# Sixteen small SBUF to SBUF copies on two queues in place of a trip through DRAM, in a hybrid attention step

## The reference, cut to what matters

```
z = h @ w_in                                   # split into q, k, v, gate of both mixers
s = einsum('bqhcd,bshcd->bhcqs', q, k) / sqrt(64)
p = softmax(s)
p = p[:, :, 0] - lam * p[:, :, 1]              # one block of probabilities for a head
o = einsum('bhqs,bshe->bqhe', p, v)            # then RMS norm, gate, and o @ w_out
```

## Time and profile before

| | |
|---|---|
| median of 3 runs | 1240.4 us (1240.19 to 1240.67) |
| the profiled execution: its time, its span | 1241.58 us, 1239.8 us |
| granted TensorE clock, mean | 0.995 |
| TensorE busy | 1205.5 us, 97% of the span |
| VectorE, ScalarE, GpSimd busy | 824.4, 595.7, 259.4 us (66%, 48%, 21%) |
| DMA, mean rate | 144 GB/s |
| transfers to `p_spill`, from `p_spill` | 28 and 112 |

### The profile page before, as it was taken

One profiled execution on the slowest core, in us unless ns is written; L12 is line 12 of the kernel. 1 busy time (PEld: TensorE's weight loads), 2 busy tenths in 40 slices (PEclk: granted clock), 3 DMA queues, 4 the chain that ended last, 5 costly groups with the idle time before them and its releaser, 6 DMA issues.

```text
span 1239.8 us, 16738 instructions
## 1 busy us (share of the span) xinstructions
PE 1205.5 (97%) x6083; PEld 975.4 (79%) x6083; DVE 824.4 (66%) x1270; ACT 595.7 (48%) x1268; POOL 259.4 (21%) x439
## 2 busy tenths in 40 slices
PE   5899999999999999999999999999999899999996
PEld 3555788888888888888888888888888778888885
DVE  4445488677677686765757575666657674879774
ACT  5522234546546455565555555564656555312223
POOL 1211033003031040222222222222223312210111
PEclk9999999999999999999999999999999999999998
DMA  9999242122132232344343434243445623756544
GB/s 352 372 376 362 85 111 77 43 70 97 55 103 60 68 94 65 90 135 122 110 124 111 130 104 140 84 145 103 138 122 163 187 84 110 249 189 225 187 135 178
DMA packets 150643, 178.46 MB, mean 144 GB/s; under 512 B 10545, under 2 KB 113617, under 8 KB 149793
## 3 DMA queue, kind: packets, MB, share of 16 engines
q1 hardware_dynamic: 136688, 131.63, 32.9%
q0 software_dynamic: 13424, 45.20, 11.5%
q10 hardware_dynamic: 448, 0.57, 0.1%
HBM read 155.19 MB, written 22.17 MB: 143 GB/s over the span
## 4 chain that ended last, share of the span: by engine, by line
PE 91%; SPq 3%; DVE 2%; DMA 1%; issue 1%; ACT 1%; POOL 1%; ACTq 0%; DVEq 0%; POOLq 0%
PE z_ps L753 24%; PE z_ps L755 24%; PE z_ps L754 24%; PE ring L844 4%; PE ring L935 4%; SPq L684 2%; PE ring L779 2%; PE ring L939 2%; PE ring L878 2%; PE ring L877 2%; DMA ada_raw<-in_w_ada_dram 1%; PE ring L755 1%; PE ring L754 1%; PE ring L942 1%; PE ring L753 1%
## 5 line engine op out<-in xcount | busy, mean ns | idle before, releaser
L753 PE MATMUL z_ps<-w_hi,xt_hi 128*128 128x512 f32 x1350 | 549.4, 407 | 2.2 <-issue 1.1
L755 PE MATMUL z_ps<-w_hi,xt_lo 128*128 128x512 f32 x1350 | 527.3, 391 | 0.0
L754 PE MATMUL z_ps<-w_lo,xt_hi 128*128 128x512 f32 x1350 | 526.8, 390 | 0.0
L1058 ACT ACTIVATE w_hi<-w_raw 128x512 fp32r<-128x512 f32 x270 | 169.5, 629 | 345.5 <-PE z_ps L755 331.0
L1511 DVE TENSOR_TENSOR w_lo<-w_raw,w_hi 128x512 fp32r<-128x512 f32 x270 | 196.6, 731 | 171.2 <-ACT w_hi L1058 170.6
L753 PEld LDWEIGHTS z_ps<-w_hi,xt_hi 128*128 128x128 f32 x1350 | 254.0, 188 | 70.0 <-issue 27.1
L755 PEld LDWEIGHTS z_ps<-w_hi,xt_lo 128*128 128x128 f32 x1350 | 253.4, 188 | 55.1
L754 PEld LDWEIGHTS z_ps<-w_lo,xt_hi 128*128 128x128 f32 x1350 | 254.7, 189 | 41.0
L1612 DVE TENSOR_REDUCE small<-s_sb 128x2 f32<-128x1536 f32 (+1 forms) x60 | 88.1, 1468 | 23.9 <-ACT s_sb L1058 23.9
L1223 ACT ACTIVATE s_sb<-s_sb,small 128x768 f32<-128x768 f32 (+1 forms) x120 | 98.0, 820 | 3.5 <-DVE small L1612 3.5
L1983 POOL TENSOR_TENSOR sg<-sg,zs 128x128 f32<-128x128 f32 (+1 forms) x60 | 38.0, 634 | 266.5 <-DVE sg L1581 266.0
(11 more groups left out here) (197 smaller groups left out, 1359.7 us busy)
## 6 DMA issues: line engine op xcount, KB each, us to landing
w_raw<-in_w_in_dram SPq DMA_DIRECT2D x188, 256.0 KB, 3.2
ada_raw<-in_w_ada_dram SPq DMA_DIRECT2D x64, 512.0 KB, 11.3
w_raw<-in_w_out_dram SPq DMA_DIRECT2D x64, 256.0 KB, 3.6
gate_raw<-in_w_ada_dram POOLq DMA_DIRECT2D x12, 1024.0 KB, 8.2
p_spill<-s_sb SPq DMA_DIRECT2D x28, 384.0 KB, 2.3
p_blocks<-p_spill SPq DMA_DIRECT2D x112, 96.0 KB, 2.2
w_raw<-in_w_in_dram POOLq DMA_DIRECT2D x20, 256.0 KB, 6.3
o_spill<-row_st POOLq DMA_DIRECT2D x14, 320.0 KB, 3.0
```

Source lines behind the costliest of these rows:

```text
L753: pe.matmul(out, hi_l, hi_r, start=start, stop=False)
L754: pe.matmul(out, hi_l, lo_r, start=False, stop=False)
L755: return pe.matmul(out, lo_l, hi_r, start=False, stop=stop)
L1058: return act.activation(out, in_, ACT.Copy, **kw)
```

## The change

`move_blocks` no longer goes through DRAM. It copies from `s_sb` to `p_blocks` inside SBUF, one transfer for each pair of a 32-partition group of the source and one of the destination: 16 transfers of 32 x 192 values (24 KB) for a tile. Eight are issued by SyncE, where the five transfers were, and eight by GpSimd, one step after the scores' step, after `gate_mul` and `o_root` of that step and ahead of its `load_row`. The waits on the spilled block go; VectorE's `turn_blocks` and ScalarE's `scores_out`, which frees `s_sb` two tiles later, now wait for all 16 transfers.

```diff
--- before.py
+++ after.py
@@ -309,7 +309,6 @@
     gv_v = cache_gqa_v[0, 0].rearrange("(j p) h d -> p j h d", p=P)
     o_spill = nc.dram_tensor("o_spill", (H_A + H_B, P, TILES * P), F32).ap()
     gate_rows = nc.dram_tensor("gate_rows", (2, D_MODEL), F32).ap()
-    p_spill = nc.dram_tensor("p_spill", (2, P, NKEY), F32).ap()
 
     at = [(nc.sbuf_base + 31) // 32 * 32]
 
@@ -443,7 +442,7 @@
         max_ready, exp_done, p_ready = sem("max_ready"), sem("exp_done"), sem("p_ready")
         pt_hi_done = sem("pt_hi_done")
         p_turned = sem("p_turned")
-        p_out, p_in = ([sem(f"{w}{b}") for b in range(2)] for w in ("p_out", "p_in"))
+        p_in, p_in_pool = ([sem(f"{w}{b}") for b in range(2)] for w in ("p_in", "p_in_pool"))
         o_part, o_sq, o_rstd, og_ready = sem("o_part"), sem("o_sq"), sem("o_rstd"), sem("og_ready")
         gr_ready = sem("gr_ready")
         row_out, row_in = ([sem(f"row_{w}{b}") for b in range(2)] for w in ("out", "in"))
@@ -651,6 +650,24 @@
                     eng.dma_start(dst[:, u, :], wo_v[:, MIX[s + u], c0:c0 + NCOL]).then_inc(landed, 16)
 
 
+        def move_blocks(eng, a, t, quadrants, landed):
+
+            b, n = t % 2, p_count(a, t)
+            eng.wait_ge(p_ready, n_step(a, t) + 1)
+            if n > 1:
+                eng.wait_ge(p_turned, turns_before(a, t) - 1)
+            else:
+                wait_full(eng, TURN[("V", D_IT - 1, TILES - 1)])
+            for i in quadrants:
+                for j in range(QUAD):
+                    src = s_sb[SUB * j:SUB * (j + 1), b, 0, KB * SUB * i:KB * SUB * (i + 1)]
+                    eng.dma_start(p_blocks[b][SUB * i:SUB * (i + 1), j, :], src).then_inc(landed[b], 16)
+
+        def wait_blocks(eng, a, t):
+
+            for landed in (p_in, p_in_pool):
+                eng.wait_ge(landed[t % 2], 16 * QUAD * QUAD // 2 * p_count(a, t))
+
         def h_copies(eng_copy, eng, t, odd):
 
             for g in range(odd, HT_GROUPS, 2):
@@ -697,20 +714,6 @@
                 load_x(t)
             for n in range(ADA_LOADS[0], sum(ADA_LOADS)):
                 load_ada(n)
-            def move_blocks(a, t):
-
-                b, n = t % 2, p_count(a, t)
-                sp.wait_ge(p_ready, n_step(a, t) + 1)
-                sp.dma_start(p_spill[b], s_sb[:, b, 0, :]).then_inc(p_out[b], 16)
-                if n > 1:
-                    sp.wait_ge(p_turned, turns_before(a, t) - 1)
-                else:
-                    wait_full(sp, TURN[("V", D_IT - 1, TILES - 1)])
-                sp.wait_ge(p_out[b], 16 * n)
-                for i in range(QUAD):
-                    src = p_spill[b].rearrange("(j b) (i n) -> i b j n", j=QUAD, i=QUAD)[i]
-                    sp.dma_start(p_blocks[b][SUB * i:SUB * (i + 1), :, :], src).then_inc(p_in[b], 16)
-
             j = EARLY_PAIRS
             for q in range(OPEN, len(ORDER)):
                 moves = [(a, t) for kind, a, t in steps_at(*ORDER[q - 1]) if kind == "S" and by_blocks(a, t)]
@@ -719,7 +722,7 @@
                         load_w(sp, j)
                         j += 1
                 for a, t in moves:
-                    move_blocks(a, t)
+                    move_blocks(sp, a, t, range(0, QUAD // 2), p_in)
             for j in range(j, ITS * KT // 2):
                 load_w(sp, j)
             for t in range(TILES - 1):
@@ -1177,12 +1180,12 @@
                 if group_kind(a) == "G" and t == 0:
                     act.wait_ge(zr_ready, a + 1)
                 if t == 0 and a > D_IT:
-                    act.wait_ge(p_out[0], 16 * p_count(a - 1, 4))
+                    wait_blocks(act, a - 1, 4)
                 if t == 1 and a > D_IT:
-                    act.wait_ge(p_out[1], 16 * p_count(a - 1, 3))
+                    wait_blocks(act, a - 1, 3)
                 if by_blocks(a, t):
                     if t > 2:
-                        act.wait_ge(p_out[t % 2], 16 * p_count(a, t - 2))
+                        wait_blocks(act, a, t - 2)
                     for c_ in range(2):
                         wait_full(act, n + c_)
                         copy(quads(s_sb[:, t % 2, c_, :])[:, 0:LAT],
@@ -1631,7 +1634,7 @@
             def turn_blocks(a, t):
 
                 b = t % 2
-                dve.wait_ge(p_in[b], 16 * QUAD * p_count(a, t))
+                wait_blocks(dve, a, t)
                 wait_full(dve, TURN[("V", a, t - 1)])
                 dve.transpose(pt_f[:, :].rearrange("p (k j b) -> p j k b", k=KB, j=QUAD),
                               p_blocks[b][:, :, :].rearrange("p j (k b) -> p j k b", k=KB)).then_inc(p_turned, 1)
@@ -2061,7 +2064,7 @@
                                ).then_inc(gate_in[gate_unit(cc, 4 * q) % 2], 16)
 
             load_kv(0)
-            late = []
+            late, turning = [], []
             for it, s in ORDER:
                 c_step = chore_step(it, s)
                 if 0 < it <= OUT_IT:
@@ -2116,6 +2119,9 @@
                         spill(a)
                     if kind == "V" and t == TILES - 1:
                         o_root(a, t)
+                for kind, a, t in turning:
+                    move_blocks(pool, a, t, range(QUAD // 2, QUAD), p_in_pool)
+                turning = [(kind, a, t) for kind, a, t in late if kind == "S" and by_blocks(a, t)]
                 late = [step for step in late if step[0] != "V" or step[2] < TILES - 1]
                 if it == OUT_IT - 1 and s >= ROW_LAG - 1:
                     load_row(s - (ROW_LAG - 1))
```

## The result

The changed kernel takes 1261.36 us (1260.83 to 1262.46, four executions) against 1240.54 of the kernel before on the same chip: ratio 1.0169, 95% interval 1.0152 to 1.0187. It is slower by 20.8 us; the forecast was 17.3 us, 1257.7, with a range of 1250 to 1267.

What follows compares the result with a forecast made beforehand. TensorE bounds ordinary heads, so they cost 0; in iteration 12 late rows hold it. Four groups of 4.3 us less 1.6 give 15.6, plus 1.7 for the clock: 17.3 us, 1257.7 us, range 1250 to 1267.

Steps and rivals of the forecast that it cites:

- The mechanism: In iteration 12, eight issues on GpSimd ahead of each `load_row` delay rows ScalarE already awaits; four groups add 17.2 us.
- The group of eight: On GpSimd's queue, the eight new issues for one tile take 4.3 us (0.64 + 7 x 0.52).
- The bounds 4.0 and 6.2: Lowest and highest price in us of eight issues on GpSimd; the upper is 8 x 0.77.
- The 112 issues: Sign in the changed profile if right: 112 issues on GpSimd of about 0.52 us.
- upper price bound of 1266: Upper end, in us, of the kernel time that the price bounds alone gave; the lower was 1254.8.
- the dearer rival: VectorE holds up GpSimd's descriptions, each issue costs 0.77 us; 27.9 us in all, 1268.3 us; chance 0.20.
- 1.6 us of waiting for blocks: In iteration 12, the turn of tile 4 waited 1.61 us for blocks; this disappears inside the delay, leaving 15.6 us.
- V of tile 4: In iteration 12, late by four groups of 4.3 us less the 1.6 us block wait: 15.6 us.
- The clock: After the fourth TensorE wait in iteration 12, a stretch partly at 1.2 GHz is not absorbed: +1.7 us.
- all four waits would be followed by one: By the skill's rule, each TensorE wait of about 5 us in iteration 12 brings a half-rate stretch; the sum stays.
- Ordinary heads: In six heads GpSimd's blocks land before TensorE needs V, with 1.1 us margin at tile 4: cost 0.
- SyncE was taken at 3.5 us for eight: SyncE's eight issues take 2.6 to 3.5 us, its half landing 5.3 us after `p_ready`: no cost, no gain.

## Why the prediction was right, and what it mis-sized

**The mechanism** was the forecast's: not the copies, but eight issues in GpSimd's queue ahead of `load_row`. Issues without use did it (17.2 us), the same issues in the six heads ahead did nothing (1.0002), moving the row took it away, and head 11 alone carried it (1.0003 without it). In iteration 12 itself the issues without use cost 14.3 us and the change 18.3; the wait of 2.98 us, which that run lacks, is most of the difference.

**The group of eight** was put at 4.3 us and is 4.0. Four make 16.1 us, 1.1 less than in the sum. The bounds 4.0 and 6.2 held it at the lower end. The 112 issues named among the signs are a miscount: 28 tiles with eight are the 224 of the view. The range's upper price bound of 1266 is not worked out there either; by its own terms (four groups of 6.2, less 1.6, and 1.7) it is 1265.3. The Trainium skill's page "SBUF — State Buffer" ("Who interferes with whom") states that GpSimd cannot write descriptors while VectorE holds both port pairs, and stood beside the dearer rival; these traces show GpSimd's issues at 498 ns in the median and 598 at most beside a VectorE busy for two thirds of the time, so the lock is not seen here. Whether any of VectorE's instructions used both pairs, no row shows.

**The unexplained wait** was in no term: 2.98 us ahead of the second group. It is between the first row's lateness (3.6 us) and the second's (9.9), whose difference of 6.3 us is one group, 4.0, and most of that wait. Four groups and the wait are 19.1 us; the last row is 17.9 late. That 1.6 us of waiting for blocks would disappear in the delay holds roughly: V is late by 15.8, 2.1 less than the row. So V of tile 4 is 15.8 us late for a forecast of 15.6 by luck: 3.0 us of wait that the sum did not have are met by 1.1 of cheaper groups, 1.2 that did not reach the last row, and 0.5 more made up behind it.

**The clock** was put at 1.7 us, one stretch of 3.4 at half rate. It is a stretch of 6.8 us at the last V, up to 3.4 us of work, and what was left of it in the time is, by subtraction, 18.3 - 15.8 = 2.5. The stretches at the first two V were absorbed, as the prediction said: from the second row to the fourth the lateness grows by 3.9 and 4.1 us, one group each and no more. The page "TensorE: Matmul & The Clock Gate" of the Trainium skill, Part 1, states that after standing idle the engine runs at 1.2 GHz, and the rows show such stretches at the waits of 3.2, 5.0 and 4.0 us. That all four waits would be followed by one did not hold: they were 3.2, 5.0, 1.9 and 4.0 us and not near 5 each, and the third V, after 1.9 us, ran at full rate (1.57 us).

**The end** was left out: 2.5 us of GpSimd's drain. In the total it is the largest error, since the wait was made up for by other terms. Together: 17.3, with 0.2 for V of tile 4 (15.8 for 15.6), 0.8 for the clock and 2.5 for the end, less the 0.65 by which this profile was ahead before iteration 12, make 20.15 for the spans' 20.2.

**Ordinary heads** cost 0, as worked out, though by less than I thought: the last of GpSimd's blocks for tile 2 landed 10.2 to 11.1 us after ready, where the forecast was 8.8 (690.5 less 681.66) and VectorE's turn had stood at 9.5, and VectorE and ScalarE waited for them. It stayed under TensorE's own work. For tile 4 GpSimd's last block landed after 6.2 to 6.5 us, as forecast (6.4).

**SyncE** was taken at 3.5 us for eight and needs 5.0. Its half of tile 4 landed after 6.2 to 6.7 us and not 5.3, as late as GpSimd's. It cost nothing at eight. At sixteen it is the bound, and there my expectation failed by a factor of three: it priced one group and not the queue that four groups make.

**What stays open.** What GpSimd waits for in the 2.3 to 3.0 us without a releaser, and what makes its drain long. Neither was settled. The wait stands ahead of the 202nd and the 312th transfer of GpSimd's queue, at quite different instructions, in six kernels: the changed one and the runs with the row ahead, the issues in heads 5 to 10, the row first after the change, and head 11 on the old way with the row last or first. Sixteen or thirty-two more transfers moved it elsewhere. The drain was 5.2 to 5.4 us in kernels without small issues in iteration 12 (6.1 where heads 5 to 10 had copies on GpSimd), 6.48 with 16, 7.8 to 8.1 with 32 there. Why the clock fell behind some waits and not behind others of the same length is open too.

## What to carry to other kernels

Before work is put on a queue that has time to spare, look up what stands behind it in that queue and whether the engine that waits for that is already waiting: if so, each group of issues is paid whole, and the share of busy time (21% for GpSimd) says nothing on it. The cure can be the order: a transfer issued at the head of its step undid 20 us here, and gave the kernel before 2.6 us. Price a queue as a queue, since where one burst does not end before the next is due, the lateness is carried from burst to burst (3.2, 5.2 and 3.4 us on SyncE with sixteen issues).

## What the runs showed of the hardware

Copies of 24 KB inside SBUF cost 498 ns of GpSimd's queue and 591 of SyncE's each, landing 1.8 us after issue. GpSimd's queue stood still for 2.3 to 3.0 us at a few places, in six kernels at the same counts of its transfers (202 and 312) and at different instructions. Its drain at the end of the program took from 5.2 to 8.1 us; in these kernels SyncE's ends some 5.5 us after it begins, and what exceeds that is time of the kernel. TensorE fell to 1.2 GHz at waits of 2.1 to 5.0 us in these kernels, for 3.4 or 6.8 us, but not at all of them: with the row ahead of the group a wait of 3.2 us was followed by no such stretch, nor was one of 2.5 us with thirty-two transfers more.
